# Differential attention's output with tokens on partitions: row sums by ScalarE, one scale per token, one turn for both halves

## What is computed

```python
def one_block(args):                       # 128 queries at a time
    ...
    s = jnp.einsum('bqhcd,bkhcd->bhcqk', qb, k) * scale        # c = 0, 1
    p = jax.nn.softmax(jnp.where(mask, s, -jnp.inf), axis=-1)
    a = p[:, :, 0] - lam * p[:, :, 1]
    return jnp.einsum('bhqk,bkhe->bqhe', a.astype(v.dtype), v)
...
o = rms_norm(o, subln_g, SUBLN_EPS) * (1.0 - lambda_init)      # over the 128 dims of a head
return o.reshape(B, S, DIFF_HEADS * DIFF_V_DIM) @ w_o
```

## Time and profile before

| | |
|---|---|
| median of 3 runs | 3088.03 us (3085.23 to 3092.97) |
| profiled execution | 3083.29 us, its span 3081.5 us |
| TensorE busy | 2970.5 us (96%), weight loads 2324.9 us |
| VectorE, ScalarE, GpSimd busy | 1424.4, 1316.5, 1325.8 us |
| stage of the change | about 2241 to 2521 us of the span: loop from 2280, tail from 2483 |

### The profile page before, as it was taken

One profiled execution on the slowest core, in us unless ns is written; L12 is line 12 of the kernel. 1 busy time (PEld: TensorE's weight loads), 2 busy tenths in 40 slices (PEclk: granted clock), 3 DMA queues, 4 the chain that ended last, 5 costly groups with the idle time before them and its releaser, 6 DMA issues.

```text
span 3081.5 us, 39504 instructions
## 1 busy us (share of the span) xinstructions
PE 2970.5 (96%) x13676; PEld 2324.9 (75%) x13676; DVE 1424.4 (46%) x2118; ACT 1316.5 (43%) x2002; POOL 1325.8 (43%) x637
## 2 busy tenths in 40 slices
PE   7999999999998899999998999999989999999998
PEld 4667888878875678888766877888867788778886
DVE  5444555225627535541496335232178863433322
ACT  4555444334456434442455335443243443443422
POOL 4213444444456344444686424444433343344443
PEclk8999999999999999999999999999999999999999
DMA  4112233332220132333223213233322232223332
GB/s 139 47 31 79 89 95 94 97 102 91 94 76 1 55 110 89 95 96 102 82 69 106 85 45 104 91 95 96 103 86 67 69 106 68 74 90 95 91 100 89
DMA packets 77090, 261.53 MB, mean 85 GB/s; under 512 B 9392, under 2 KB 9520, under 8 KB 76720
## 3 DMA queue, kind: packets, MB, share of 16 engines
q1 hardware_dynamic: 74320, 253.61, 27.0%
q10 hardware_dynamic: 2016, 3.81, 0.3%
q0 software_dynamic: 640, 2.62, 0.3%
HBM read 256.86 MB, written 2.10 MB: 84 GB/s over the span
## 4 chain that ended last, share of the span: by engine, by line
PE 63%; issue 19%; POOL 9%; DVE 4%; ACT 3%; DMA 1%; POOLq 0%; DVEq 0%; SPq 0%; ACTq 0%
PE bank L852 16%; PE bank L853 16%; PE bank L854 16%; POOL w_lo L698 8%; PE bank L880 1%; PE bank L981 1%; PE bank L881 1%; PE bank L882 1%; PE bank L1336 1%; ACT c_pr L2688 1%; DVE bank L2069 1%; PE bank L1025 1%; PE bank L1024 1%; PE bank L1026 1%; DVE acc L2160 1%
## 5 line engine op out<-in xcount | busy, mean ns | idle before, releaser
L698 POOL TENSOR_TENSOR w_lo<-w_raw,w_hi 128x1024 fp32r<-128x1024 f32 (+1 forms) x449 | 1032.6, 2301 | 1492.2 <-ACT w_hi L2346 1492.2
L2346 ACT ACTIVATE w_hi<-w_raw 128x1024 fp32r<-128x1024 f32 (+1 forms) x499 | 506.1, 1016 | 665.9 <-DMA w_raw<-w_glu_out 152.7
L852 PE MATMUL bank<-xh,w_hi 128*128 128x512 f32 x1736 | 691.8, 399 | 1.1 <-DVE xl L1559 1.0
L853 PE MATMUL bank<-xl,w_hi 128*128 128x512 f32 x1736 | 688.2, 396 | 0.0
L854 PE MATMUL bank<-xh,w_lo 128*128 128x512 f32 x1736 | 688.1, 396 | 0.0
L852 PEld LDWEIGHTS bank<-xh,w_hi 128*128 128x128 f32 x1736 | 327.0, 188 | 83.5 <-DVE xl L1559 2.8
L853 PEld LDWEIGHTS bank<-xl,w_hi 128*128 128x128 f32 x1736 | 327.0, 188 | 80.4 <-issue 1.4
L854 PEld LDWEIGHTS bank<-xh,w_lo 128*128 128x128 f32 x1736 | 327.0, 188 | 79.8
L854 PE MATMUL bank<-hh,w_lo 128*128 128x512 f32 x704 | 279.1, 396 | 0.0
L852 PE MATMUL bank<-hh,w_hi 128*128 128x512 f32 x704 | 279.1, 396 | 0.0
L853 PE MATMUL bank<-hl,w_hi 128*128 128x512 f32 x704 | 279.1, 396 | 0.0
(11 more groups left out here) (356 smaller groups left out, 4960.4 us busy)
## 6 DMA issues: line engine op xcount, KB each, us to landing
w_raw<-w_ffn_in SPq DMA_DIRECT2D x88, 512.0 KB, 3.5
w_raw<-w_glu_in SPq DMA_DIRECT2D x88, 512.0 KB, 3.5
w_raw<-w_ffn_out SPq DMA_DIRECT2D x48, 512.0 KB, 3.5
w_raw<-w_glu_out SPq DMA_DIRECT2D x48, 512.0 KB, 3.5
w_raw<-w_ssm_in SPq DMA_DIRECT2D x41, 512.0 KB, 3.5
w_raw<-w_pw SPq DMA_DIRECT2D x24, 512.0 KB, 3.6
w_raw<-w_diff_in SPq DMA_DIRECT2D x24, 512.0 KB, 3.5
w_raw<-w_attn_in SPq DMA_DIRECT2D x18, 512.0 KB, 3.5
```

The costliest lines, as they stand in the source:

```text
L698: pool.tensor_tensor(w_lo[:, slot, 0:n], w_raw[:, slot, 0:n], w_hi[:, slot, 0:n].bitcast(F32), ALU.subtract).then_inc(w_split, 1)
L852: pe.matmul(b, wh, hi[:, k, 0:n], start=(k == 0), stop=False)
L853: pe.matmul(b, wh, lo[:, k, 0:n], start=False, stop=False)
L2346: act.activation(w_hi[:, slot, 0:n], w_raw[:, slot, 0:n], ACT.Copy).then_inc(w_half, 1)
```

## The change

The product with the values swaps its operands: the turned probabilities are stationary and the values move, so bank 5 has 128 tokens on partitions and the 128 dimensions along the free dimension, once for each of the 4 token tiles. `square` is cut into four instructions of 128 columns that also write the sum along the free dimension to a column of `o_r`; `out`, on TensorE, is gone. The root is taken by ScalarE right behind `square(7)`, ahead of the tail's first slabs, and waits there for ScalarE's own 32 sums. `diagonal`, `spread` and `normed` are gone. In their place `scaled(g)` multiplies each token tile of `d_q` in place by its reciprocal (4 instructions of 128 x 128 on VectorE), `turn_out(g)` transposes the 4 tiles into bank 4 or 7 on TensorE, and `upper` and `lower` both read that bank and scale by `sub_out`, the gain times 1 - lambda_init, which VectorE makes once at the start of the stage. `turn_out(g)` stands behind chunk g + 9, one chunk earlier than `spread(g)` did, and waits for `scaled(g)` and from g = 2 for `lower(g - 2)`. `upper` begins at c = 10 instead of 11. On VectorE `lower(g - 1)` comes ahead of the eviction of chunk g + 10.

```diff
@@ -255,7 +255,7 @@
         lam_t = d_q[:, 1, 0:128].rearrange("p (a n) -> p a n", a=2)
         lam_e = sb("lam_e", [P, 4])
         o_r = sb("o_r", [P, NT * KD])
-        o_diag = a_pt_t
+        sub_out = sb("sub_out", [P, 1])
         pos_i = d_v[:, 0, :].bitcast(I32)
         d_t = d_v[:, 1:3, :]
         d_turn = sq[:, 1, :]
@@ -554,8 +554,7 @@
         lam_in, lam_sum, lam_exp = sem("lam_in"), sem("lam_sum"), sem("lam_exp")
 
         r_clear = sem("r_clear")
-        o_dia, o_bc = sem("o_dia"), sem("o_bc")
-        o_raw, o_sq, o_sum, o_root, o_new = (sem(n) for n in ("o_raw", "o_sq", "o_sum", "o_root", "o_new"))
+        o_raw, o_sq, o_root, o_new, o_turn = (sem(n) for n in ("o_raw", "o_sq", "o_root", "o_new", "o_turn"))
 
 
         c_gate, c_sig, c_dia, c_pe, c_step, c_done, c_out = (
@@ -1188,25 +1187,18 @@
                             pe.wait_ge(o_raw, h)
                     pe.wait_ge(a_pt, t0 + m + 1)
                     for v, kt, _, _, _, t in units[2 * m].pv:
-                        mm = pe.matmul(bank[5][:, t * P:(t + 1) * P], v, a_pt_t[:, m % 2, kt * P:(kt + 1) * P],
+                        mm = pe.matmul(bank[5][:, t * P:(t + 1) * P], a_pt_t[:, m % 2, kt * P:(kt + 1) * P], v,
                                        start=(kt == 0), stop=(kt == t), skip_group_check=True)
                     mm.then_inc(a_pv, 1)
 
-                def out(g):
-
-                    pe.wait_ge(o_sq, g + 1)
+                def turn_out(g):
+
+                    pe.wait_ge(o_new, g + 1)
+                    if g >= 2:
+                        pe.wait_ge(a_ol, g0 + g - 1)
                     for t in range(NT):
-                        mm = pe.matmul(NORM_BANK[:, NT * g + t:NT * g + t + 1], sq[:, 0, t * P:(t + 1) * P],
-                                       ones[:, 0:1], start=True, stop=True, skip_group_check=True)
-                    mm.then_inc(o_sum, 1)
-
-                def spread(g):
-
-                    pe.wait_ge(o_dia, g + 1)
-                    if g >= 2:
-                        pe.wait_ge(o_new, g - 1)
-                    pe.matmul(bank[4 + 3 * (g % 2)][:], ones[:], o_diag[:, g % 2, :], start=True, stop=True)\
-                        .then_inc(o_bc, 1)
+                        mm = pe.transpose(bank[4 + 3 * (g % 2)][:, t * P:(t + 1) * P], d_q[:, g, t * P:(t + 1) * P], ident[:])
+                    mm.then_inc(o_turn, 1)
 
                 def turn_memory(c):
 
@@ -1236,22 +1228,16 @@
                     feed(n)
                     if m >= 2:
                         outputs(m - 2)
-                    if i == 3 and 2 <= s <= KD:
-                        out(s - 2)
                     feed(n)
                 feed(8 * 4 * KD)
                 work = memory_values()
                 for c in range(KD, 2 * KD):
                     feed(8)
-                    if c == KD:
-                        out(KD - 1)
-                    else:
+                    if c > KD:
                         turn_memory(c - 1)
-                    if c >= KD + 2:
-                        spread(c - KD - 2)
+                        turn_out(c - KD - 1)
+                turn_out(KD - 1)
                 turn_memory(2 * KD - 1)
-                spread(KD - 2)
-                spread(KD - 1)
                 vt[0] += 2 * KD
                 au[0] += 2 * DM
                 at[0] += DM
@@ -1794,24 +1780,19 @@
                     dve.wait_ge(a_pv, t0 + NT * (g + 1))
                     dve.tensor_copy(d_q[:, g, :], bank[5][:]).then_inc(o_raw, 1)
 
-                def diagonal(g):
-
-                    if g >= 2:
-                        dve.wait_ge(o_bc, g - 1)
-                    r = o_r[:, NT * g:NT * g + NT].unsqueeze(2).broadcast_to([P, NT, P])
-                    dve.tensor_tensor(o_diag[:, g % 2, :].rearrange("p (a n) -> p a n", n=P),
-                                      ident[:].unsqueeze(1).broadcast_to([P, NT, P]), r, ALU.mult).then_inc(o_dia, 1)
-
-                def normed(g):
-                    dve.wait_ge(o_bc, g + 1)
-                    dve.scalar_tensor_tensor(d_q[:, g, :], d_q[:, g, :], col("subln"), bank[4 + 3 * (g % 2)][:],
-                                             ALU.mult, ALU.mult).then_inc(o_new, 1)
+                def scaled(g):
+
+                    for t in range(NT):
+                        o = d_q[:, g, t * P:(t + 1) * P]
+                        ins = dve.tensor_scalar(o, o, o_r[:, NT * g + t:NT * g + t + 1], None, ALU.mult)
+                    ins.then_inc(o_new, 1)
 
                 def lower(g):
                     dve.wait_ge(a_oh, g0 + g + 1)
-                    dve.scalar_tensor_tensor(ol[:, g, :], d_q[:, g, :], 1.0 - LAMBDA_INIT, oh[:, g, :].bitcast(F32),
+                    dve.scalar_tensor_tensor(ol[:, g, :], bank[4 + 3 * (g % 2)][:], sub_out[:], oh[:, g, :].bitcast(F32),
                                              ALU.mult, ALU.subtract).then_inc(a_ol, 1)
 
+                step(dve.tensor_scalar(sub_out[:], col("subln"), 1.0 - LAMBDA_INIT, None, ALU.mult))
                 dve.memset(d_rot, 0.0).then_inc(r_clear, 1)
                 for c in range(KD):
                     dve.wait_ge(y_hi, c + 1)
@@ -1850,15 +1831,14 @@
                 evict(4 * KD + 1)
                 dve.wait_ge(o_root, 1)
                 step(dve.reciprocal(o_r[:], o_r[:]))
-                diagonal(0)
+                scaled(0)
                 for g in range(KD):
                     if g + 1 < KD:
-                        diagonal(g + 1)
+                        scaled(g + 1)
+                    if g:
+                        lower(g - 1)
                     if g + 2 < KD:
                         evict(4 * KD + g + 2)
-                    normed(g)
-                    if g:
-                        lower(g - 1)
                 lower(KD - 1)
                 vt[0] += 2 * KD
                 au[0] += 2 * DM
@@ -2471,10 +2451,10 @@
 
                 def square(g):
                     act.wait_ge(o_raw, g + 1)
-
-                    if g:
-                        act.wait_ge(o_sum, g)
-                    act.activation(sq[:, 0, :], d_q[:, g, :], ACT.Square).then_inc(o_sq, 1)
+                    for t in range(NT):
+                        ts = slice(t * P, (t + 1) * P)
+                        act.activation(sq[:, 0, ts], d_q[:, g, ts], ACT.Square, accum_out=o_r[:, NT * g + t:NT * g + t + 1])\
+                            .then_inc(o_sq, 1)
 
                 def memory_value(c):
 
@@ -2484,8 +2464,8 @@
                         .then_inc(v_ready, 1)
 
                 def upper(g):
-                    act.wait_ge(o_new, g + 1)
-                    act.activation(oh[:, g, :], d_q[:, g, :], ACT.Copy, scale=1.0 - LAMBDA_INIT)\
+                    act.wait_ge(o_turn, g + 1)
+                    act.activation(oh[:, g, :], bank[4 + 3 * (g % 2)][:], ACT.Copy, scale=sub_out[:])\
                         .then_inc(a_oh, 1)
 
                 for c in range(KD):
@@ -2517,20 +2497,18 @@
                 while turned[0] < 4 * KD + 1:
                     next_slab()
                 square(KD - 1)
+                act.wait_ge(o_sq, NT * KD)
+                act.activation(o_r[:], o_r[:], ACT.Sqrt, scale=1.0 / P, bias=eps[:, 1:2]).then_inc(o_root, 1)
                 for c in range(KD, 2 * KD):
                     next_slab()
                     next_slab() if c < KD + 2 else None
-                    if c == KD + 1:
-                        act.wait_ge(o_sum, KD)
-                        act.activation(o_r[:], NORM_BANK[:, 0:NT * KD], ACT.Sqrt, scale=1.0 / P, bias=eps[:, 1:2])\
-                            .then_inc(o_root, 1)
                     if c > KD:
                         memory_value(c - 1)
-                    if c >= KD + 3:
-                        upper(c - KD - 3)
+                    if c >= KD + 2:
+                        upper(c - KD - 2)
+                upper(KD - 2)
+                upper(KD - 1)
                 memory_value(2 * KD - 1)
-                for g in range(KD - 3, KD):
-                    upper(g)
                 vt[0] += 2 * KD
                 au[0] += 2 * DM
                 at[0] += DM
```

## The result

| | before | after |
|---|---|---|
| median of 12 runs | 3088.28 us (3079.55 to 3093.14) | 3094.24 us (3091.31 to 3103.21) |
| ratio after to before | | 1.0027, 95% interval 1.0017 to 1.0038 |
| profiled execution, its span | 3083.29, 3081.5 us | 3103.21, 3101.4 us |
| first score to last turn of probabilities | 201.07 us | 201.11 us |
| last turn of probabilities to the projection | 39.86 us | 46.46 us |

By the ratio the change made the kernel slower by 8.3 us (5 to 12); the two medians are 6.0 us apart. 3091.9 was forecast, with 3084 to 3099 as its range.

A forecast was written before the change was run, and what follows sets the result against it. VectorE was taken to set the end of each loop head, ScalarE and GpSimd the tail's start. Terms 0.2 + 6.3 + 1.6 - 2.15 - 2.05 = +3.9 took the median from 3088.03 to 3091.9 us, range 3084 to 3099.

The forecast's parts named there:

- The bound in the loop: Loop heads: VectorE sets their end, so removing TensorE's sums gains 0; the wait grows from 0.30 to about 1.1 us.
- The root ahead of the slabs: Tail's start: squares, table load and root on ScalarE come before the slabs, so chunk 9 starts 2.65 us later.
- the prediction's other estimate: Tail's start: by the skill's fixed cost per instruction alone, the four squares would make chunk 9 2.2 us late.
- The scaled tile behind GpSimd's block: First turn in the tail: `scaled(0)` waits for GpSimd's four slabs to end; +6.3 so far, 2.65 of it from the slabs.
- The clock: Behind TensorE's idle time ahead of the first turn: one more fall, 3.2 us at half speed, +1.6; bounds 0 and twice that.
- The end of the tail: From chunk 15 to the projection: 5.5 us before, 3.45 after, with `lower(5)` at 3.0; -2.05.
- Each later chunk: Tail chunks after the first turn: each loses the spread (0.86) and gains the turn (0.43); 5 periods, -2.15.
- `scaled` is held in each chunk: Rival, tail: GpSimd's slab holds a scaling in every chunk, 2.1 us each time; +10.6 in all, 3098.6 us; chance 0.15.
- the clock falls in the loop: Rival, loop heads: six waits of 1.1 us each bring a half-speed fall; some +13, 3101 us; chance 0.06.

## Why the prediction was right, and where it was off

*The bound in the loop* was right and is shown: 201.11 for 201.07 us, waits of 1.20 for the 1.1 worked out, and the work put back costs nothing.

*The root ahead of the slabs* was right in kind, +2.3 for +2.65. The squares with sums take 0.29 us from start to start (2496.19 to the third at 2496.48), not the 0.39 of the Exp from PSUM in the earlier trace rows; the slabs started 2.28 us later for it all, nearer to the 2.2 of the prediction's other estimate than to its 2.65. The table load was 1.28 as in the earlier trace rows.

*The scaled tile behind GpSimd's block* was right: the first turn waits 2.73 us, about 3 were forecast, and ends its wait with the block.

*The clock* was a term that was too small. The fall behind the first turn was taken as 3.2 us at half speed, +1.6; it held for all of 2509.8 to 2515.9, +2.7. With the same wait it lasted as long in two further executions and about half as long in a third, so that 1.6 was one of its sizes and not the usual one. A second one at the projection was not foreseen at all (+1.5 there, +0.5 on the last turn and on L1212), because I read the step before it wrongly.

*The end of the tail* is the step that failed: "-2.05", measured +0.4 (5.12 us from chunk 15 to the projection before, 5.52 after). I had the chain right (slab, `upper(5)`, `lower(5)`, turn) but had `lower(5)` done 3.0 us behind chunk 15; the turn behind it started at 4.35 (2533.55 to 2537.90). The slab of this chain took 4.69 us to land, where the median of the tail's slabs is 3.6. Of the 2.45 us, 1.35 are this and 0.5 the clock. The other 0.6 are a slip of reading: the start of the projection before was taken from the chain, 2521.17, and the timeline has it at 2520.60, so there was less to gain. That moving `upper` ahead of the slab takes 2.1 us off this wait shows that the chain is the cause.

*Each later chunk* lost 0.43 as forecast.

*The rivals.* That `scaled` is held in each chunk did not happen in the kernel after the change (0.87 us for four), and did in most chunks of two of the reordered ones, where an eviction and a `lower` (about 1 us) stand ahead of it. That the clock falls in the loop did not happen in the heads with waits of 1.20. It did fall in the next to last head, before the change as after it (granted clock 0.86 and 0.93), behind a pause of TensorE of 1.93 us, and cost nothing there: the head took 23.89 and 23.90 us. In three kernels without that fall (all of the order moved, and the two with the new operations and the copy on ScalarE) the last head began with a wait of 3.77 to 3.79 us and lost 1.6 to 2.8 us at a granted clock of 0.88 to 0.93, so this rival's mechanism exists, at another place than it was put.

The forecast of the sign held, its size, +3.9, is under the interval of +5 to +12. The time stands within the range because the range took in the held scalings, not because their cause came true. In that the number is luck; the sign and the path up to the end of chunk 15 are not.

## The clock and the spread of the runs

What I had not expected is how much of everything is the clock. For 29 runs of the kernel before, made with the later experiments, the product of span and mean granted clock is 3034.5 us in the mean, and span and clock are correlated at -0.92: the longer executions, up to 3096 us, are those with the lower clock, and the shorter ones, down to 3079, those with the higher. The 12 runs after the change have 3034.6 for the product. The mean clock is 0.9835 before (29 runs) and 0.9809 after, 0.26% less, about 8 us. So the product, which counts a wait at full clock like work, did not change by more than about 1 us, and the runs' loss shows as a lower clock. In the trace the tail's granted clock falls from 0.96 to 0.83 (from the last turn of probabilities through the projection's first four tiles). The version with scaled tiles two ahead has 3030.4 for the product, 4 us less than before, and a clock of 0.9826 that gives most of it back. The clock is recorded in thousandths, each worth 3 us, so that this is a reading of means only.

What a wait brings is not fixed by its length. The waits of the tail in all profiled kernels, with the time that the work behind them took:

| the wait ahead of | its length, us | the work behind it, and what it takes at full speed |
|---|---|---|
| chunk 9, order of before | 1.25, 1.18 | 4.44, 2.94 (2.94) |
| chunk 9, root behind four slabs | 2.68, 2.68, 2.59, 2.69 | 2.94, 2.95, 2.95, 4.45 (2.94) |
| chunk 9, root early | 4.22 to 4.34, seven times | 4.40 to 4.45 five times, 5.16, 5.26 (2.94) |
| the first turn, right behind chunk 9 | 2.71, 2.73, 2.79, 2.72 | 6.04, 6.03, 6.02, 4.72 with chunk 10 (3.36) |
| the first turn, behind a fast chunk 9 and behind a slow one | 4.03, 1.66 | 4.86, 3.36 (3.36) |
| `turn_memory(10)`, with scaled tiles two ahead and the copy moved | 2.61 | 3.59 with turn and chunk, no fall |
| the last turn | 3.54, 3.24, 2.66 | down at once; the projection's first four tiles 4.76, 4.84, 5.27 (2.88) |
| the same | 3.37, 3.23, 1.95 | down within the projection: 4.43, 4.42, 4.41 (2.88) |
| the same | 2.84, 2.29, 1.40, 1.09 | 2.88 to 2.89, no fall (2.88) |
| the last two turns, one chunk later | 2.13 and 1.03 | down at once, 4.27 (2.88) |
| the last spread, order of before | 2.04, 2.20 | 3.22, 4.77 (3.22 with the spread's end) |

So a wait of 1.2 us brought a fall in one execution and none in another, and waits of 2.6 to 2.8 did either as well. Each of the twelve waits from 3.2 to 4.3 us in this table was followed by one. What sets the start and the length of a fall stays open.

## What to carry to other kernels

Before work is taken from the busiest engine, look for a wait on it in the same stretch: a wait of 0.30 us at each head's start, released by a chain that never pauses, said that 0.81 us of removed products would be worth nothing, and it was so to 0.1 us. Operations that are moved between engines are cheap or dear by what is queued behind them: here the table load and root ahead of four slabs, and a rounding behind a slab that had not landed, were worth 4.3 and 2.7 us of the tail when each was moved alone. Waits on TensorE like those of 2.7 and 3.5 us here can cost up to their length once more through the clock; the sum of a forecast should have both cases. Putting the consumer one chunk later was worth 4.0 us, and is worth trying before finer tuning.
